# Mixture-of-experts tiles of 32 slots instead of 64, turned by VectorE instead of TensorE, and a new last normalisation

## What is computed

```python
def post_norm(x, y, gate, g, b):
    return layer_norm(DEEPNORM_ALPHA * x + gate * y, g, b)

def moe(h, w_router, b_router, w_gate, w_up, w_down):   # sigmoid router, best group of 4, top 2 in it
    ...
    hid = jax.nn.silu(jnp.einsum('bld,edf->blef', h, w_gate)) * jnp.einsum('bld,edf->blef', h, w_up)
    y = jnp.einsum('blef,efd->bld', hid * combine[..., None].astype(hid.dtype), w_down)

# one layer's end:  x = post_norm(x, moe(modulate(x, ml[3], ml[4]), ...), ml[5], ln_g[i, 1], ln_b[i, 1])
```

## Time and profile before

| | |
|---|---|
| runs | 901.22 us median of 3 (898.92 to 905.03) |
| profiled execution, its own time | 900.66 us |
| its span, first to last instruction | 898.8 us |
| time around the span | 1.86 us |
| mean granted PE clock | 0.909 |
| mixture of layer 0, first gate/up to last scatter issued | 131.1 to 292.7 us |
| mixture of layer 1, the same | 748.5 to 871.6 us |
| last norm, from the results' load to the end of the span | 873.3 to 898.8 us |

### The profile page before, as it was taken

The page is one execution under the profiler, slowest core; times in us unless marked ns, Lnnn a source line. Parts: engine busy times, 40 slices in busy tenths (PEclk is TensorE's granted clock), DMA queues, the critical chain, the costliest instruction groups (busy, mean ns, idle before and its releaser), DMA issues. The chain is left out here.

```text
span 898.8 us, 15497 instructions
## 1 busy us (share of the span) xinstructions
PE 740.8 (82%) x5225; PEld 431.1 (48%) x5225; DVE 477.4 (53%) x1089; ACT 316.9 (35%) x778; POOL 300.1 (33%) x702
## 2 busy tenths in 40 slices
PE   0988879999997177999999999999898547999950
PEld 0544435555553023556666566665655233555520
DVE  1048654533334583643767777777744753443326
ACT  0240322222222225644657566575641121222211
POOL 0000113443344000366164846648440012434330
PEclk9989969999999569995999999999997857999985
DMA  9999999999990899576152442522110299999912
GB/s 250 408 394 393 411 412 406 408 408 346 359 390 25 326 367 261 186 205 209 41 145 52 108 124 53 142 60 100 43 60 1 104 403 392 404 405 407 376 65 112
DMA packets 107239, 219.34 MB, mean 244 GB/s; under 512 B 28293, under 2 KB 63437, under 8 KB 102817
## 3 DMA queue, kind: packets, MB, share of 16 engines
q1 hardware_dynamic: 98207, 200.39, 61.9%
q0 software_dynamic: 8224, 15.76, 4.6%
q10 hardware_dynamic: 740, 2.32, 0.9%
HBM read 212.09 MB, written 17.33 MB: 255 GB/s over the span
## 5 line engine op out<-in xcount | busy, mean ns | idle before, releaser
L1234 PE MATMUL banks<-h_cols,weight_ring 128*128 128x512 f32 (+1 forms) x384 | 160.3, 538 | 0.7
L1211 POOL TENSOR_TENSOR arena<-arena 128x60 f32<-128x60 f32 (+24 forms) x248 | 81.8, 330 | 123.3 <-DMA arena<-blocks 104.5
L1213 POOL TENSOR_TENSOR arena<-arena 128x60 f32<-128x60 f32 (+24 forms) x248 | 84.0, 339 | 19.4
L903 POOL DMA_INDIRECT y_of_tokens<-arena,place_now x42 | 47.3, 1126 | 127.9 <-ACT arena L795 127.9
L747 PE MATMUL banks<-arena 128*64 128x512 f32 x352 | 85.2, 605 | 3.0 <-DVE arena L839 3.0
L1234 PEld LDWEIGHTS banks<-h_cols,weight_ring 128*128 128x128 f32 x384 | 66.2, 194 | 34.7 <-issue 31.7
L875 POOL DMA_INDIRECT arena<-h_of_tokens,row_now x50 | 53.1, 1063 | 80.7 <-DVE token_of_slot L715 35.3
L287 PE MATMUL banks<-weight_ring,c_cols 128*32 128x512 f32 x368 | 52.3, 687 | 29.3 <-DMA weight_ring<-in_w_mod_dram 29.3
L765 PE MATMUL banks<-weight_ring,arena 128*64 128x256 f32 x576 | 67.6, 388 | 0.9 <-DVE arena L827 0.9
L831 DVE TENSOR_TENSOR arena<-arena,banks 128x128 f32<-128x128 f32 x42 | 12.1, 288 | 102.8 <-ACT arena L800 102.8
L800 ACT ACTIVATE arena<-banks 128x128 f32<-128x128 f32 x42 | 11.7, 278 | 143.1 <-PE banks L765 143.1
(11 more groups left out here) (291 smaller groups left out, 1374.7 us busy)
## 6 DMA issues: line engine op xcount, KB each, us to landing
weight_ring<-in_w_mod_dram SPq DMA_DIRECT2D x46, 1024.0 KB, 9.9
weight_ring<-in_dn_w_in_dram SPq DMA_DIRECT2D x32, 512.0 KB, 7.0
weight_ring<-in_w_gate_dram SPq DMA_DIRECT2D x13, 1024.0 KB, 10.5
weight_ring<-in_w_up_dram SPq DMA_DIRECT2D x13, 1024.0 KB, 14.6
weight_ring<-in_w_down_dram SPq DMA_DIRECT2D x13, 1024.0 KB, 15.5
arena<-in_w_gate_dram SPq DMA_DIRECT2D x7, 1024.0 KB, 12.5
arena<-in_w_up_dram SPq DMA_DIRECT2D x7, 1024.0 KB, 14.6
arena<-in_w_down_dram SPq DMA_DIRECT2D x7, 1024.0 KB, 16.3
```

The costliest lines, as they stand in the source:

```text
L903: pool.indirect_dma_start(y_halves, bass.IndirectOffsetOnAxis(m.place_now[:, u:u + 1], 0), v.y_tile[u], None, bounds_check=last_row, oob_i ...
L1211: then(pool.tensor_tensor(part, U[:, 0:q, j:j + 1].to_broadcast([P, q, BLK - 1 - j]), M[:, j, j + 1:BLK].unsqueeze(1).to_broadcast([P, q, ...
L1213: ins = pool.tensor_tensor(U[:, 0:q, j + 1:BLK], U[:, 0:q, j + 1:BLK], part, ALU.subtract)
L1234: mm = pe.matmul(bank(6 + j % 2)[:, 0:CTX + SEQ - n0], head_w[h % 2][:, j, k, :], m.hT[:, k, n0:CTX + SEQ], start=(k == 0), stop=(k == KD ...
```

## The change

Tiles have 32 slots. A fetch brings 128 quarter rows of 1 KB; slot s has its four quarters on partitions s, 32+s, 64+s and 96+s. There are four buffers for rows and four for results, and rows are fetched six tiles ahead. Gate/up and down run in four groups of 32 columns of PE: gate/up is 8 steps of four matmuls of 128 columns (64 records), down is 2 steps of four matmuls of 256 columns (16 records). DVE turns both operands in blocks of 32x32, straight from SBUF to SBUF, and PE turns nothing. The tiles are filled up to a multiple of four, now with empty tiles of the first expert, so there are 40 and 28. The weights' rows are laid out with `(p k)`, one run of 8 KB. In layer 1 the copy of w_down is a multiplication with GATE2 (both operands in SBUF). The end of layer 1 has x scaled by alpha ahead, adds both results of a token with a weight each, makes the sum of the last 128 rows on PE with diagonal matrices, and stores in halves.

```diff
-TILE = 64
-TILES = 36
+TILE = 32
+TILES = 56
+QUARTER = D // 4
...
-                    sp.dma_start(whole[slot][:, a, :].rearrange("p (j n) -> p j n", j=2),
-                                 w.rearrange("(j p k) f -> p j (k f)", j=2, p=P)).then_inc(done, 16)
+                    sp.dma_start(whole[slot][:, a, :], w.rearrange("(p k) f -> p (k f)", p=P)).then_inc(done, 16)
...
             def down():
                 for f in range(FC):
-                    for h in range(2):
-                        mm = pe.matmul(column_half(B_DOWN, h), v.hidden[:, f, :], v.down_now[:, f, h * BANK:(h + 1) * BANK],
+                    for g in range(4):
+                        mm = pe.matmul(group(B_DOWN, g)[:, 0:QUARTER], v.hidden[:, f, :], v.down_now[:, f, g * QUARTER:(g + 1) * QUARTER],
                                        start=(f == 0), stop=(f == FC - 1))
...
                     for k in range(KD):
-                        if k == KD - 1:
-                            pe.wait_ge(s(t_ + "rows_copied"), q + 2)
-                        for h in range(2):
-                            mm = pe.matmul(column_half(B_GU, h)[:, 0:2 * P], v.slots_T[:, k, :], gate_up(slot, k)[:, :, h * P:(h + 1) * P],
+                        for g in range(4):
+                            mm = pe.matmul(group(B_GU, g)[:, 0:P], v.slots_T[:, k, :], gate_up(slot, k)[:, :, g * HALF:(g + 1) * HALF],
                                            start=(k == 0), stop=(k == KD - 1))
...
-                    turn().then_inc(s(t_ + "turned"), 1)
...
-                    pe.transpose(m.ps[:, B_HID, 0:P], v.hid_rows, v.ident).then_inc(s(t_ + "hid_turned"), 1)
...
             def turned():
-                dve.tensor_copy(v.slots_T.rearrange("p (h k) n -> p h (k n)", h=2), turned_rows).then_inc(s(t_ + "slots_T"), 1)
+                dve.transpose(v.slots_T, v.rows.rearrange("p (n k) -> p k n", k=KD)).then_inc(s(t_ + "slots_T"), 1)
 
             def tile(e, q):
+                dve.wait_ge(s(t_ + "gate_up"), q + 1)
+                dve.wait_ge(s(t_ + "rows_copied"), q + 2)
+                turned()
                 dve.wait_ge(s(t_ + "silu"), q + 1)
-                dve.tensor_tensor(v.hid_rows, v.silu, m.ps[:, B_GU, P:2 * P], ALU.mult).then_inc(s(t_ + "hid_rows"), 1)
-                dve.wait_ge(s(t_ + "turned"), q + 1)
-                turned()
-                dve.wait_ge(s(t_ + "hid_turned"), q + 1)
+                dve.wait_ge(s(t_ + "hidden"), q + 1)
+                dve.tensor_tensor(v.hid_rows, v.silu, m.ps[:, B_GU, HALF:P], ALU.mult).then_inc(s(t_ + "hid_rows"), 1)
                 dve.wait_ge(s(t_ + "down"), q + 1)
-                dve.tensor_copy(v.hidden.rearrange("p f n -> p (f n)"), m.ps[:, B_HID, 0:P])
+                dve.wait_ge(s(t_ + "hid_rows"), q + 1)
+                dve.transpose(v.hidden, v.hid_rows.rearrange("p (n f) -> p f n", f=FC))
                 dve.wait_ge(*expert_loaded(L, e))
                 for to, of in down_pieces(expert_slot(L, e)):
-                    ins = dve.tensor_copy(to, of)
+                    if L.n == 0:
+                        ins = dve.tensor_copy(to, of)
+                    else:
+                        to, of = (x.rearrange("p (c n) -> p c n", n=D) for x in (to, of))
+                        ins = dve.tensor_tensor(to, of, mod_vec(GATE2).unsqueeze(1).to_broadcast([P, to.shape[1], D]), ALU.mult)
                 ins.then_inc(s(t_ + "hidden"), 1)
...
+            def tile(j, u, first=False):
+                n = 4 * j + u
+                b = (u + 2) % 4
+                if not first:
+                    pool.wait_ge(s(t_ + f"y_stored{u}"), 16 * j)
+                pool.tensor_copy(m.place_now[:, u:u + 1], m.place_of[:, bass.ds(n, 1)]).then_inc(s(t_ + "place_now"), 1)
+                pool.wait_ge(s(t_ + "rows_copied"), n + 3)
+                pool.tensor_copy(m.row_now[:, b:b + 1], m.token_of[:, bass.ds(n + 6, 1)]).then_inc(s(t_ + "row_now"), 1)
+                pool.wait_ge(s("h_stored"), 16 * (L.h_base + L.tiles))
+                pool.wait_ge(s(t_ + "row_now"), n + 3)
+                rows(b, b)
+                pool.wait_ge(s("router_table"), 3 * L.n + 3)
+                pool.wait_ge(s(t_ + "place_now"), n + 3)
+                pool.wait_ge(s(t_ + "y_tile"), n + 3)
+                pool.indirect_dma_start(y_quarters, bass.IndirectOffsetOnAxis(m.place_now[:, u:u + 1], 0), v.y_tile[u], None,
+                                        bounds_check=last_row, oob_is_err=False).then_inc(s(t_ + f"y_stored{u}"), 16)
...
+        def pe_last_sum(pe):
+            t = XT - 1
+            pe.wait_ge(s("x_scaled"), XT + 2)
+            for half in range(2):
+                pe.matmul(m.ps[:, 3 + half, :], v.ident, m.x[:, L1.x_tiles[t], half * BANK:(half + 1) * BANK], start=True, stop=False)
+            pe.wait_ge(s(f"y_back{t % 2}"), 32 * 3)
+            for c in range(2):
+                for half in range(2):
+                    mm = pe.matmul(m.ps[:, 3 + half, :], weight_diag[c], v.back[:, t, c, half * BANK:(half + 1) * BANK],
+                                   start=False, stop=(c == 1))
+            mm.then_inc(s("y_mixed"), 1)
```

More of the change, by code:

```diff
@@ new lines, in pool_moe @@
+            for name in ("row_now", "place_now"):
+                pool.sem_inc(s(t_ + name), 2)
+            for u in range(4):
+                tile(0, u, True)
+            with pool.Fori(1, quads) as j:
+                for u in range(4):
+                    tile(j, u)
+            for u in range(4):
+                pool.wait_ge(s(t_ + f"y_stored{u}"), 16 * quads)
+            pool.sem_inc(s("y_drained"), 1)
+            for u in range(4):
+                pool.wait_ge(s(t_ + f"rows{u}"), 16 * quads + (32 if u < 2 else 16))
@@ new lines, in dve_last_norm @@
+        def dve_last_norm(dve, t):
+            c = LN_BASE["ln1b_"] + t
+            x = m.x[:, L1.x_tiles[t], :]
+            if t < XT - 1:
+                dve.wait_ge(s("x_scaled"), XT)
+                dve.wait_ge(s(f"y_back{t % 2}"), 32 * 3)
+                dve.scalar_tensor_tensor(out=x, in0=v.back[:, t, 0, :], scalar=v.weights[:, 0, t:t + 1], in1=x, op0=ALU.mult,
+                                         op1=ALU.add).then_inc(s("ln_gated"), 1)
+                dve.wait_ge(s("ln_gated"), c + 1)
+                dve.scalar_tensor_tensor(out=x, in0=v.back[:, t, 1, :], scalar=v.weights[:, 1, t:t + 1], in1=x, op0=ALU.mult,
+                                         op1=ALU.add).then_inc(s("ln_summed"), 1)
+                dve.wait_ge(s("ln_summed"), c + 1)
+            else:
+                dve.wait_ge(s("y_mixed"), MT + 1)
+                x = last_sum()
+            for half in range(2):
+                dve.bn_stats(v.stats[:, 2 * (t % 2) + half, :], x[:, half * BANK:(half + 1) * BANK]).then_inc(s("ln_stats"), 1)
+            dve.wait_ge(s("ln_stats"), 2 * c + 2)
+            dve.bn_aggr(v.mean_var[:, t, 0:2], v.stats[:, 2 * (t % 2):2 * (t % 2) + 2, :]).then_inc(s("ln_var"), 1)
@@ L2200, in _ @@
             act_moe(act, L1)
-            act_moe_norms(act, L1, "ln1b_")
+            for t in range(XT):
+                act_std(act, "ln1b_", t)
         @block.tensor
@@ L2260, in _ @@
             pe_moe(pe, L1)
+            pe_last_sum(pe)
         @block.vector
```

244 lines of the change are left out of this document (127 added, 117 removed).

## The result

The changed kernel took 932.31 us, median of 4 runs (929.26 to 934.94); before took 901.32 beside it. The ratio is 1.0331, with a 95% interval of 1.0294 to 1.0369: 3.3% slower. The forecast was 922.0, its own range 908 to 946. The profiled execution has a span of 933.1 us, before 898.8, so 34.3 us are to be accounted for.

What follows compares the result with a forecast made beforehand. POOL's work per tile was expected to bound the kernel: 900.66 + 11.0 (layer 0) + 14.8 (layer 1) - 4.7 (end) = 921.8, said as 922 us. The forecast's own range was 908 to 946, the whole range 874 to 946.

Steps and rivals of the forecast that it cites:

- Layer 1's step, 4.70 us: POOL's time per tile in layer 1, with starts delayed by DVE's multiplication: 4.70 us, near its lower bound of 4.6.
- Layer 0's step, 4.16 us: POOL's time per tile in layer 0: 3.55 us plus half of DVE's 1.22 us copy, 4.16.
- the prediction's other value, 4.35: Layer 0's step if DVE's copy also held up descriptors of a DMA under way: 4.35 us, total 7 us higher.
- So PE would allow 3.0 us in layer 0: PE's cost per tile: gate/up 2.0 plus down 0.94, 2.96 us, with turns gone from PE.
- The 3.6 us for VectorE in layer 1: DVE's operations per tile in layer 1: sum 3.3 us, about 3.6 with the waits for down between.
- Rival 1 (880 us): DVE's operations miss POOL's starts, or POOL's sequence is shorter; layer 0 at 3.55, layer 1 follows the stream; chance 0.35.
- Turn of rows: DVE's turn of a tile's rows: like L1494, 256 columns, 435 ns.
- The other 0.25s: DVE's multiplication of 64 columns and turn of 64 columns per tile: each taken as 0.25 us.
- First scatters: First scatter about 9.4 us after the first gate/up in layer 0, at 140.5; about 10 in layer 1, at 758.5.
- The end, -4.7 us: After layer 1's last tile: 6.6 us saved, 1.3 lost to PE's sum, 0.6 to extra POOL hops; net 4.7 gained.
- The middle, 0: From layer 0's last scatter to layer 1's first gate/up: no change, 0 us.
- The signs: Right: steps 4.2 and 4.7, held fetches and copies. Wrong: scatters waiting for ACT, stream full to 853, last scatter near 867.

Runs made afterwards that it cites:

- e3_psum: Changed kernel with VectorE's operation on the down weights made a multiplication by a vector in PSUM in both layers; 926.4 us, ratio 1.026 to before.
- e15_no_copy: Changed kernel with VectorE's operation on the down weights cut to 32 columns, rest constants, GATE2 missing; 918.8 us, ratio 1.018 to before.
- e9_half_gu: Changed kernel with every second k of gate/up left out, 32 records in place of 64; 914.5 us, ratio 1.014 to before.
- e6_pool_more: Changed kernel with two more 128x1 column copies on POOL in every tile of both layers; 938.8 us, ratio 1.038 to before.
- e8_pe_loads: Changed kernel with TensorE's two register loads of the next expert's count moved behind the tile loop; 941.9 us, ratio 1.043 to before.
- e16_short_turn: e15_no_copy with VectorE's row turn cut to two of its eight blocks of 32 columns; 928.4 us, ratio 1.026 to before.
- e2_new_end: Kernel before with only the new end, including layer 1's down weights multiplied by GATE2, on its 64-slot tiles; 900.1 us, ratio 0.996 to before.
- e1_old_end: Changed kernel with before's end and layer 1's down weights copied, not multiplied by GATE2; 922.5 us, ratio 1.021 to before.

## Why the prediction was right, and where it was not

The total was inside the forecast's own range and on its side, 10 us short. Part of that is luck: the prediction had TensorE's limit in layer 0 at 3.0 us, it was 4.25, and it happened to be as long as POOL's step and no longer. Step by step:

- **Layer 1's step, 4.70 us.** Right in size (4.78) and in cause: the lower bound of the prediction's own reckoning is what the steady tiles show. e3_psum and e15_no_copy, without the lock, fall to 4.41 and 4.33. e9_half_gu and the 0.28 us of e6_pool_more say the same: here POOL holds the step. But the reckoning would have taken them to 3.6; what taking the lock away gives is 0.4 us, not 1.15.
- **Layer 0's step, 4.16 us.** Near in size (4.32) and half right in cause. POOL's fetches are held by a copy that begins under way, and the prediction's other value, 4.35, is closer. But POOL isn't alone: e15_no_copy has the same mean of 4.32 with the lock all but gone. Two circles of 4.2 us each ran side by side.
- **"So PE would allow 3.0 us in layer 0".** This is the step that failed. 2.0 for gate/up and 1.07 for down (forecast 0.94) are right by the records, but a sum of busy times isn't a cycle. The turn of the next rows waits for gate/up, and the next gate/up waits for the turn: +0.85. From the multiplication's end to the next gate/up TensorE takes +0.6; it stays in e8_pe_loads, so it isn't the register loads, and what it is made of isn't shown. And gate/up ends 0.8 late where POOL issues a DMA. 2.0 + 0.8 + 0.85 + 0.6 = 4.25. The 3.6 us for VectorE in layer 1 failed in the same way: with the lock gone the steps there are 4.41 (e3_psum).
- **Rival 1 (880 us).** It was given 0.35. Its condition, no blocked start, was all but met in e15_no_copy and in e3_psum, and they took 919 and 926 us: with these circles it would not have come true.
- **VectorE.** Turn of rows 0.644, not 0.435: 256 columns on 128 partitions with a strided source are not the 32 partitions of the earlier trace rows. The other 0.25s (0.18 and 0.25), the copy (1.19) and the multiplication (2.25) fit. The turn stands in TensorE's circle, so its 0.2 us too much are part of the 4.25; but cutting it (e16_short_turn) gained nothing, since gate/up then ended later.
- **First scatters.** 141.74 (forecast 140.5); in layer 1 11.1 us behind the first gate/up (forecast 10).
- **The end, -4.7 us.** -4.3 in after, -3.4 by the ratio of e2_new_end. The term was slightly oversized: TensorE's sum is ready 9.14 us after VectorE's start (917.02 to 926.16), not 8.0. The larger miss is that the prediction booked the gain here and the price of the same idea, VectorE's longer operation in layer 1, under the tiles: taken together the new end costs the new kernel some 10 us (e1_old_end).

```profile
917.02 1.28 DVE L966 SCALAR_TENSOR_TENSOR x_rows<-arena,small,x_rows 128x1024 f32<-128x1024 f32 x1 [16.99 <-DMA arena<-y_of_tokens]
...
926.20 1.29 DVE L976 BATCH_NORM_STATS2 small<-banks 128x6 f32<-128x512 f32 x2 [2.09 <-PE banks L956]
```

- **The middle, 0.** +5.1 us in this profile, most likely by the granted clock; not by a step of the change.
- **The signs.** The steps of 4.2 and 4.7 and the held fetches and copies came as named. The 11 scatters that wait for ACT and the full stream of layer 1 up to 875 us were on the side of wrong, and the experiments bear them out so far: POOL is a bound in both layers, but not the only one.

Still open: why gate/up in four column groups ends late when an indirect DMA is issued beside it, and whether the issue is the cause. In before, with gate/up in two groups, SiLU starts 3.72 us behind the first record in 40 of 42 tiles (the others are the first of each layer), though POOL starts an indirect DMA inside 38 of the 40. Whether a version of after with the issues placed between gate/ups would run at 3.5 us a step wasn't tried.

## What to carry to other kernels

Before you take an engine's busy sum for what it would allow, draw the circle of waits through all engines for one tile, with every single buffer in it: a buffer written between two uses by the same engine puts the writer's time, and the loop's own instructions, into the step. When a step is made short, fixed costs that don't shrink with it (an indirect DMA's 1 us, a lock, a branch) come to set it, and several limits then stand close together, so that taking one away gains little: test with one more and one less of each, and believe neither alone. And of a change in two parts, time each alone and each on top of the other: here the new end gained 3.4 us on the old tiles and lost 10 on the new ones, and the tiles alone (e1_old_end) lost some 19.

## What was not expected of the hardware

- A gate/up of 64 fp32 matmuls in four column groups lets SiLU start 2.02 us after its first record when POOL issues nothing (3.65 in one such tile), and 2.6 to 3.0 (median) when an indirect DMA of POOL is under way during it, 4.06 with two close together. In about half of these cases its records end at 1.95 all the same, so the page's busy time doesn't show it. In two column groups of the kernel before there is no such delay: 3.72 us with and without.
- A VectorE copy of 128x2048 that begins 0.5 us inside an indirect DMA's issue stretches it from 1.04 to some 1.82 us (1.77 to 1.86 in 13), and isn't held itself; a multiplication of the same size with one input in PSUM does not (maximum 1.29).
- A small cut can cost: 0.34 us less VectorE in the circle made the kernel 7 to 10 us slower (918.8 to 928.4; 7.4 by the ratios to before), and POOL relieved of two copies made it 66 us slower than e3_psum.
